# The experts' loop of a mixture-of-experts layer: weight matrices fetched whole, gate and up in turn over both column halves

## The reference, cut to what is computed

```python
    def expert_block(args):
        xblk, e = args
        hid = jax.nn.silu(xblk @ w_gate[e]) * (xblk @ w_up[e])
        return hid @ w_down[e]

    yb = lax.map(expert_block, (xb, blk_expert)).reshape(n_buf, d)
    out = jnp.zeros((n_tok, d), jnp.float32).at[buf_tok].add(yb.astype(jnp.float32) * buf_w[:, None])
```

## Time and profile before

| | |
|---|---|
| median of 3 runs | 2854.72 us (2854.51 to 2856.84) |
| the profiled execution, its own time | 2857.5 us |
| its span, first to last instruction | 2855.7 us |
| mean granted TensorE clock | 0.992 |
| PE busy / weight loads / DVE / ACT | 95% / 77% / 51% / 20% of the span |
| bytes moved | 588.76 MB, of which the experts' 258 transfers of 1024 KB are nearly half |

### The profile page before, as it was taken

The page is one execution under the profiler, slowest core; times in us unless marked ns, Lnnn a source line. Parts: engine busy times, 40 slices in busy tenths (PEclk is TensorE's granted clock), DMA queues, the critical chain, the costliest instruction groups (busy, mean ns, idle before and its releaser), DMA issues. The chain is left out here.

```text
span 2855.7 us, 42346 instructions
## 1 busy us (share of the span) xinstructions
PE 2713.9 (95%) x17366; PEld 2187.0 (77%) x17366; DVE 1455.8 (51%) x2804; ACT 575.2 (20%) x1121; POOL 0.2 (0%) x4
## 2 busy tenths in 40 slices
PE   8999899999999999999999999999998888888887
PEld 8998799999988999888988998888895323232322
DVE  7768678687555775544345667466323111111112
ACT  1001410010043101122010022344102222222222
POOL 0000000000000000000000000000000000000000
PEclk9999999999999999999999999999998999999999
DMA  7544145364453543545544354454542999999998
GB/s 234 207 162 149 59 150 175 133 206 160 128 141 126 172 174 117 127 115 148 165 155 153 133 133 120 134 149 132 143 142 97 423 422 422 422 422 422 422 422 332
DMA packets 382201, 588.76 MB, mean 206 GB/s; under 512 B 17088, under 2 KB 328672, under 8 KB 348896
## 3 DMA queue, kind: packets, MB, share of 16 engines
q1 hardware_dynamic: 377248, 581.92, 58.3%
q10 hardware_dynamic: 4800, 4.63, 0.5%
HBM read 585.43 MB, written 1.08 MB: 205 GB/s over the span
## 5 line engine op out<-in xcount | busy, mean ns | idle before, releaser
L3285 PE MATMUL bank<-ring,wk 128*64 128x512 f32 x1376 | 313.4, 597 | 52.3 <-DMA ring<-in_w_expert_up 49.8
L3359 DVE TENSOR_TENSOR wk<-bank,wk 64x256 f32<-64x256 f32 x86 | 52.7, 613 | 513.2 <-ACT wk L3319 511.8
L3285 PEld LDWEIGHTS bank<-ring,wk 128*64 128x64 f32 x1376 | 105.2, 137 | 252.5 <-issue 229.4
L844 PE MATMUL bank<-hR,ring 128*128 128x128 f32 x2112 | 267.7, 277 | 3.9 <-DVE hR L426 3.9
L844 PEld LDWEIGHTS bank<-hR,ring 128*128 128x128 f32 x2112 | 253.0, 194 | 4.9 <-DMA ring<-in_ffn_w_in 2.7
L3305 PE MATMUL bank<-ring,wk 128*64 128x512 f32 x688 | 157.1, 598 | 23.7 <-ACT wk L3322 23.7
L1164 PE MATMUL bank<-big,ring 128*128 128x128 f32 x1320 | 159.6, 275 | 0.0
L1164 PEld LDWEIGHTS bank<-big,ring 128*128 128x128 f32 x1320 | 153.5, 192 | 0.1
L733 PE MATMUL bank<-hR,ring 128*128 128x256 f32 x704 | 152.3, 379 | 0.0
L733 PEld LDWEIGHTS bank<-hR,ring 128*128 128x128 f32 x704 | 133.8, 190 | 18.2
L2269 PE MATMUL bank<-big,ring 128*128 128x256 f32 x640 | 141.0, 379 | 1.5 <-ACT big L2833 1.0
(11 more groups left out here) (464 smaller groups left out, 4390.1 us busy)
## 6 DMA issues: line engine op xcount, KB each, us to landing
ring<-in_ffn_w_in SPq DMA_DIRECT2D x88, 1024.0 KB
ring<-in_w_expert_gate SPq DMA_DIRECT2D x86, 1024.0 KB
ring<-in_w_expert_up SPq DMA_DIRECT2D x86, 1024.0 KB
ring<-in_w_expert_down SPq DMA_DIRECT2D x86, 1024.0 KB, 9.0
ring<-in_w_in SPq DMA_DIRECT2D x96, 512.0 KB
ring<-in_ffn_w_out SPq DMA_DIRECT2D x40, 1024.0 KB
ring<-in_w_up SPq DMA_DIRECT2D x22, 1024.0 KB
ring<-in_w_in SPq DMA_DIRECT2D x16, 1024.0 KB
```

The lines of the kernel that those rows point to most:

```text
L844: last = nc.tensor.matmul(k.bank[:, 2 * (n % 4) + p // 4, (p % 4) * P:(p % 4 + 1) * P], a[:, c, m * P:(m + 1) * P], b[:, c, :], start=c == ...
L3285: last = nc.tensor.matmul(k.bank[m * SLOTS:(m + 1) * SLOTS, self.GU, :], xg[:, c * SLOTS:(c + 1) * SLOTS], self.piece(2 * h + m)[:, (c % 4 ...
L3359: last = v.tensor_tensor(by_row, up[:, :, 2 * h:2 * h + 2], gate[:, :, 2 * h:2 * h + 2], ALU.mult)
```

## The change

Each matrix comes in one transfer of 2 MB into its own slot, in the order gate, up, down, so a block has three pieces and not six, and PE marks a piece as used after all its products. PE first multiplies with gate alone, then with up alone. Each of them now uses both column halves: columns 0 to 63 take the features 4p and 4p+1, columns 64 to 127 the features 4p+2 and 4p+3. The streamed operand is therefore a view of the slot with 2 x 128 elements in which neighbouring elements of the inner dimension lie four floats (16 bytes) apart, and a product is 256 columns wide and not 512; there are twice as many. The hidden features leave the array in the order that down needs. Gate's results lie in bank 7, up's in bank 4 (which the turning uses afterwards), each on 128 partitions x 256. ACT takes silu of gate while PE multiplies with up, out of 128 partitions. DVE multiplies with one instruction of 128 x 256, contiguous. Down's products are as before, with one wait in place of two.

```diff
--- before.py
+++ after.py
@@ -3154,7 +3154,7 @@
 
 class Experts(Stage):
 
-    PIECES = 6
+    PIECES = 3
     fence = False
 
     def name_sems(self, sem):
@@ -3178,12 +3178,11 @@
 
     WIDE = 2 * S + SLOTS
     XS, XG, Y, SI, HI, HT, GW, TM, G = 1024, 5632, 6144, 6656, 7168, 7424, 7680, 7936, 8192
-    GU, TURN, DOWN = 7, (4, 6), 5
+    GATE, UP, TURN, DOWN = 7, 4, (4, 6), 5
 
     def __init__(self, k, name, route):
         super().__init__(k, name)
         self.route = route
-        self.down_loaded = [k.sem(f"down_loaded{n}") for n in range(2)]
 
     def arrived(self, eng, n, i):
 
@@ -3192,9 +3191,7 @@
 
     def landing(self, n):
 
-        if n < NSLOT:
-            return self.k.w_loaded[n], (self.u0 - n + NSLOT - 1) // NSLOT * UNIT_INC
-        return self.down_loaded[n - NSLOT], 0
+        return self.k.w_loaded[n], (self.u0 - n + NSLOT - 1) // NSLOT * UNIT_INC
 
     def freed(self, i, n):
 
@@ -3205,7 +3202,7 @@
 
     def piece(self, n):
 
-        return self.k.ring[:, n // 2, (n % 2) * 2048:(n % 2 + 1) * 2048]
+        return self.k.ring[:, n, :]
 
     def sorted_rows(self):
         return self.w(self.XS, KC * self.WIDE).rearrange("p (c n) -> p c n", c=KC)
@@ -3220,9 +3217,9 @@
             e = sp.value_load(k.eid[0:1, bass.ds(i, 1)], min_val=0, max_val=NEXP - 1)
             gate, up, down = (k.arg[name][0][bass.ds(e, 1), :, :].rearrange("e (p a) n -> p (e a n)", p=P)
                               for name in ("w_expert_gate_3", "w_expert_up_3", "w_expert_down_3"))
-            for n, (w, h) in enumerate(((gate, 0), (up, 0), (gate, 1), (up, 1), (down, 0), (down, 1))):
+            for n, w in enumerate((gate, up, down)):
                 sp.wait_ge(k.w_used, self.freed(i, n + 1 - self.PIECES))
-                sp.dma_start(self.piece(n), w[:, h * 2048:(h + 1) * 2048]).then_inc(self.landing(n)[0], 16)
+                sp.dma_start(self.piece(n), w).then_inc(self.landing(n)[0], 16)
 
     def clear(self, pe):
 
@@ -3277,15 +3274,14 @@
         n = self.blocks(pe)
         with pe.Fori(0, n) as i:
             pe.wait_ge(self.xg_ready, i + 1)
-            for h in range(2):
-                for m in range(2):
-                    self.arrived(pe, 2 * h + m, i)
-                for c in range(4 * h, 4 * h + 4):
+            for j, bank in enumerate((self.GATE, self.UP)):
+                self.arrived(pe, j, i)
+                for c in range(KC):
+                    w = self.piece(j)[:, c * 512:(c + 1) * 512].rearrange("k (p a) -> k a p", a=4)
                     for m in range(2):
-                        last = nc.tensor.matmul(k.bank[m * SLOTS:(m + 1) * SLOTS, self.GU, :], xg[:, c * SLOTS:(c + 1) * SLOTS],
-                                                self.piece(2 * h + m)[:, (c % 4) * 512:(c % 4 + 1) * 512],
-                                                start=c == 0, stop=c == KC - 1)
-                last.then_inc(k.w_used, 2)
+                        last = nc.tensor.matmul(k.bank[m * SLOTS:(m + 1) * SLOTS, bank, 0:256], xg[:, c * SLOTS:(c + 1) * SLOTS],
+                                                w[:, 2 * m:2 * m + 2, :], start=c == 0, stop=c == KC - 1)
+                last.then_inc(k.w_used, 1)
             pe.wait_ge(self.y_taken, i + 1)
             pe.wait_ge(self.gw_ready, i + 1)
             self.put(pe)
@@ -3297,14 +3293,13 @@
                                            ident[r, r])
             last.then_inc(self.ht_ready, 1)
             pe.wait_ge(self.ht_taken, i + 1)
-            for h in range(2):
-                self.arrived(pe, 4 + h, i)
-                for c in range(2 * h, 2 * h + 2):
-                    for m in range(2):
-                        a = (c % 2) * DM + m * 512
-                        last = nc.tensor.matmul(k.bank[m * SLOTS:(m + 1) * SLOTS, self.DOWN, :], ht[:, c * SLOTS:(c + 1) * SLOTS],
-                                                self.piece(4 + h)[:, a:a + 512], start=c == 0, stop=c == 3)
-                last.then_inc(k.w_used, 1)
+            self.arrived(pe, 2, i)
+            for c in range(4):
+                for m in range(2):
+                    a = c * DM + m * 512
+                    last = nc.tensor.matmul(k.bank[m * SLOTS:(m + 1) * SLOTS, self.DOWN, :], ht[:, c * SLOTS:(c + 1) * SLOTS],
+                                            self.piece(2)[:, a:a + 512], start=c == 0, stop=c == 3)
+            last.then_inc(k.w_used, 1)
         pe.wait_ge(self.y_taken, n + 1)
         pe.wait_ge(self.gw_ready, n + 1)
         self.put(pe, final=True)
@@ -3315,12 +3310,13 @@
         act.wait_ge(self.route.eid_ready, 2)
         with act.Fori(0, self.blocks(act)) as i:
             first = act.value_load(k.first[0:1, bass.ds(i + 1, 1)], min_val=0, max_val=2 * S)
-            act.wait_ge(k.w_used, self.freed(i, 4))
-            nc.scalar.activation(self.w(self.SI, 512)[SLOTS:P, :], k.bank[0:SLOTS, self.GU, :], ACT.Silu).then_inc(self.silu_ready, 1)
+            act.wait_ge(k.w_used, self.freed(i, 1))
+            nc.scalar.activation(self.w(self.SI, 256), k.bank[:, self.GATE, 0:256], ACT.Silu).then_inc(self.silu_ready, 1)
+            act.wait_ge(k.w_used, self.freed(i, 2))
             nc.scalar.activation(self.window(), self.sorted_rows()[:, :, bass.ds(first, SLOTS)], ACT.Copy).then_inc(self.xg_ready, 1)
             act.wait_ge(self.ht_ready, i + 1)
             nc.scalar.activation(pair(self.w(self.HT, 256)), k.bank[:, self.TURN[0]:self.TURN[1] + 1:2, 0:P], ACT.Copy).then_inc(self.ht_taken, 1)
-            act.wait_ge(k.w_used, self.freed(i, 6))
+            act.wait_ge(k.w_used, self.freed(i, 3))
             nc.scalar.activation(self.w(self.Y, 512), k.bank[:, self.DOWN, :], ACT.Copy).then_inc(self.y_taken, 1)
 
     def empty(self, chain):
@@ -3351,13 +3347,10 @@
         dve.wait_ge(self.route.rows_taken, 2)
         n = self.blocks(dve)
         with dve.Fori(0, n) as i:
-            chain.enter(i, 4, [(self.hid_ready, 1), (self.gw_ready, 1)])
+            chain.enter(i, 3, [(self.hid_ready, 1), (self.gw_ready, 1)])
             dve.wait_ge(self.silu_ready, i + 1)
-            gate, up = (ap.rearrange("q (p a) -> q p a", a=4) for ap in (self.w(self.SI, 512)[SLOTS:P, :], k.bank[SLOTS:P, self.GU, :]))
-            for h in range(2):
-                by_row = self.w(self.HI, 256)[h * SLOTS:(h + 1) * SLOTS, :].rearrange("q (a p) -> q p a", a=2)
-                last = v.tensor_tensor(by_row, up[:, :, 2 * h:2 * h + 2], gate[:, :, 2 * h:2 * h + 2], ALU.mult)
-                chain(last, self.hid_ready if h else None)
+            dve.wait_ge(k.w_used, self.freed(i, 2))
+            chain(v.tensor_tensor(self.w(self.HI, 256), k.bank[:, self.UP, 0:256], self.w(self.SI, 256), ALU.mult), self.hid_ready)
             dve.wait_ge(self.put_done, i + 1)
             chain(v.scalar_tensor_tensor(gw, k.drow[:, 0:S], part, k.wrow[:, 0:S], ALU.is_equal, ALU.mult))
             chain(v.scalar_tensor_tensor(tm, k.drow[:, S:2 * S], part, k.wrow[:, S:2 * S], ALU.is_equal, ALU.mult))
```

## The result

The changed kernel takes 3101.74 us (median of 4, 3098.32 to 3104.29) beside 2854.93 us (median of 4) of the kernel before on the same chip: a ratio of 1.0862, with a 95% interval of 1.0844 to 1.0881. The forecast was 3096. The profiled execution took 3104.29 us, its span is 3102.5, so 246.8 more than the span before.

The account below looks back on a forecast made before the run. The prediction took the experts' loop as bound by its weight stream, PE having 1.2 us of cover a block. Stride +293.5 us, less 49.8 and 2.1 of waits, gave +241.6 on 2854.7: 3096 us, range 2850 to 3110.

Parts of the forecast that it names:

- What decides: Gate and up products in the experts' loop: the 16-byte stride of streamed weights slows PE, which becomes the bound; chance 0.42.
- the stride's term: Gate and up passes: each strided element costs a second column time, 427 ns a pass, 293.5 us more of PE.
- The row it was taken from: DVE's reordering product, 613 ns against 421 in order for 256 elements: 192 ns more, nearly a second column time each.
- What goes back: PE's waits in the loop that a slower PE would no longer see: 49.8 us for transfers and 2.1 for DVE.
- The term of 2.1 us: PE's wait for DVE's hidden values, 2.1 us in all, taken away by DVE's single contiguous product.
- Twice as many passes, 0: Gate and up: 64 passes of 256 columns take the same 6.83 us a half, weight loads hidden, so no cost.
- The signs named: What the profile would show in the loop: passes every 0.43 us, period near 20.4 us, DMA share near 0.73, 308 GB/s.
- Rows of 16 KB, 0: Weight stream: going from 8 to 16 KB rows with 2 MB transfers gains 0; bounds 0 and 23 us.
- the last rival: Longer rows speed up the weight stream, with a free stride: over 425.5 GB/s, down to 2832 us; chance 0.10.
- The stride is free: Gate and up: strided reading costs nothing, the loop stays with its stream, 2851 to 2858 us; chance 0.35.
- The weight loads don't hide: Gate and up, stride free: unhidden loads cost 0.17 us a pass, +182, 3037 us; part of the price, together 0.11.
- Half a column time: Gate and up: a strided element costs half a column time, +95, 2950 us; part of the price, together 0.11.

## Why the prediction was right, and where it was wrong

**What decides: right.** The forecast put the price on the stride of the streamed weights, took PE for the new bound, and expected no wait for transfers. With the stride taken away the price goes; with the stride alone in the kernel before all of it is there.

**The size of the stride's term: 293.5 us forecast, 314.6 measured** (628.0 less 313.4), 229 ns more for a pass and not 213 (314.6 / 1376). This is the term that was mis-sized. "A strided element costs a second column time" named the wrong unit: PE pays 1.77 ns for each stretch of 16 bytes entered, and with one element in each stretch that happens to be just over two column times. That the size came so near is luck. By the forecast's rule the step of 8 bytes would have cost the same 3096 us; it runs in 2849. The Trainium skill (SBUF — State Buffer, section Door 1: The DMA port swizzle) wants two hits in a line of 16 bytes for full speed; the runs agree with that half, with 0.227 us for a pass that has them and 0.216 in order. Its other half, that a step of four float32 is free, they contradict: 0.45 us against 0.216.

**The row it was taken from: near in number, not shown to be the same thing.** DVE's reordering product cost 192 ns more than one in order, and that was carried to PE. DVE's product that reads with a step of two takes 425 ns, no more than the 427 in order, so its 192 ns came with reading pairs out of four or with writing scattered. Which of the two was not tried.

**What goes back: too little.** The 49.8 us of waiting for transfers went, as forecast. The term of 2.1 us held only the part of the turning's wait that names DVE. The runs show more: its whole idle time went, from 6.4 us to 0, its busy time from 14.7 to 12.3, and down's wait for ACT from 23.7 to 20.7. The groups of turning and down before, and the turning after (down after stands above):

```profile
L3296 PE MATMUL bank<-con,wk 64*128 64x64 f32 x172 | 14.7, 240 | 6.4 <-DVE wk L3359 2.1
L3305 PE MATMUL bank<-ring,wk 128*64 128x512 f32 x688 | 157.1, 598 | 23.7 <-ACT wk L3322 23.7
...
L3292 PE MATMUL bank<-con,wk 64*128 64x64 f32 x172 | 12.3, 219 | 0.0
```

So 314.6 - 49.8 - 6.4 - 2.4 - 3.0 = +253.0, against +246.8 in the spans. Most of the rest is an overlap that this sum counts twice: after, the turning starts at 2510.07, 0.17 us before the sums end at 2510.24; before, it started behind them. That is 0.17 x 43 = 7.3 us, which leaves 1 us. The two errors, +21 in the price and -16 in what goes back, nearly cancel; that is luck too, and why 3096 came within 6 us of 3101.74.

**Twice as many passes, 0: right.** 317.4 us of products in order, against 313.4.

**The signs named: right, but one.** Passes every 0.45 us (0.43 forecast), 14.6 us of gate and up a block (13.7), a period of 20.6 (20.4; by the forecast's own sum, 14.92 + 241.6 / 43, it would be 20.5), 305 GB/s (308), the clock at 1.00, no waits for transfers. The DMA share is 0.81 where 0.73 was named; why is not shown.

**Rows of 16 KB, 0: wrong, and hidden.** The step that failed reads "from 4 to 8 KB nothing is left beyond the reading, so I take 0 for 8 to 16". Over 400 us the rates are 410, 422 and 428 GB/s. The rows of 4 KB at 419 and 424 came from windows of 2 to 4 us, as the one at 438 did; such windows do not tell 2% apart, for 438 and 421.7 were both read with rows of 8 KB. In the changed kernel PE is the bound and the gain shows nowhere, so this error cost the forecast nothing. Without the stride's price it is the whole result: ratio 0.9966 to 0.9971, the case of the last rival, at its small end. The rule that the forecast cited beside that rival from the Trainium skill (DMA: Bandwidth & Descriptors, section Bandwidth), a rate that grows with the size of a transfer, is not what the runs show: at 2 MB each, 8 KB rows run at 422, just as the queued transfers of 1 MB did. That section's table is for transfers issued from GpSimd; here SP issues them.

**The rivals.** "The stride is free" fails at 16 bytes and nearly holds at 8. "The weight loads don't hide" is excluded by the contiguous run. "Half a column time" gave 2950 us; it is what a step of 12 bytes measured, for another reason.

## What to carry to other kernels

When a float32 operand is streamed through TensorE (no other type was tried), count the stretches of 16 bytes that a pass enters, not whether the view is strided: two elements from each stretch are almost free, one costs double. If features have to be reordered, leave it to an engine whose instruction lies beside other work, as DVE's lies beside the sums here. In a loop that is bound by its transfers, make the rows in a partition longer before making the transfers larger, and read a rate from a window of hundreds of microseconds.

## What the runs showed of the hardware that was not expected

- A float32 pass takes the longer of 0.216 us for its 256 columns and 1.77 ns for each stretch of 16 bytes of the streamed operand that it enters. Steps of 8, 12 and 16 bytes gave 0.227, 0.34 and 0.45 us; a step of 32 bytes gave 640.5 us of products against 628.0 with 16.
- Two column halves with such streams side by side run as fast as one alone: 0.45 us either way.
- Where a run of passes changes from one column half to the other, about four passes of the new half ran beside the last four of the old: 64 passes of 0.45 us, with three such changes, took 23.69 us.
- The stream of weights gains from rows beyond 8 KB: 410, 422 and 428 GB/s at 4, 8 and 16 KB, which is 37.7 ns for each KB and about 9 ns for each row, if the 16 engines share it evenly.
- DVE's product of float32 read out of PSUM and SBUF with a step of two is as fast as in order, 425 ns for 256 elements.
